# A gated linear attention's projections in tiles of 128 in place of 96, inside a fused transformer kernel on one Trainium2 core

## The reference

```python
q, k, v, g, lr, mq = split_cols(xn @ gla_w_in, (4*96, 4*96, 4*192, 4*192, 16, 256))
log_a = log_sigmoid(lr @ w_gate_up + b_gate) / 16            # a decay for each head, token and key feature
# 4 heads, 96 key features and 192 value features each
#   o_t = q_t * 96**-0.5 @ S_t,   S_t = exp(log_a_t) * S_(t-1) + k_t^T v_t
o = rmsnorm(o, out_norm) * silu(g)                           # the mean square is over a head's 192 values
mo = softmax(mq @ k_mem^T * 64**-0.5) @ v_mem                # 4 heads of 64 over 256 memory rows
h = h + concat(o, mo) @ w_out                                # (256, 768 + 256) @ (1024, 1024)
```

## Time and profile before

| | |
|---|---|
| time, median of 3 runs | 1646.41 us (1645.17 to 1646.71) |
| the profiled execution: its time | 1647.83 us |
| its span, first to last instruction | 1646.0 us |
| PE busy | 1518.2 us, 92% |
| DVE busy | 938.1 us, 57% |
| ACT busy | 414.1 us, 25% |
| GpSimd busy | 597.7 us, 36% |
| mean granted clock of TensorE | 0.989 |
| moved by DMA | 421.70 MB, mean 256 GB/s |

### The profile page before, as it was taken

One profiled execution on the slowest core, in us unless ns is written; L12 is line 12 of the kernel. 1 busy time (PEld: TensorE's weight loads), 2 busy tenths in 40 slices (PEclk: granted clock), 3 DMA queues, 4 the chain that ended last, 5 costly groups with the idle time before them and its releaser, 6 DMA issues. The chain is left out here.

```text
span 1646.0 us, 22237 instructions
## 1 busy us (share of the span) xinstructions
PE 1518.2 (92%) x7776; PEld 1138.2 (69%) x7778; DVE 938.1 (57%) x2383; ACT 414.1 (25%) x1007; POOL 597.7 (36%) x524
## 2 busy tenths in 40 slices
PE   7999989999999777778799999999999999999998
PEld 6998845554455323223357788999998878799997
DVE  5652576666766876766454732555553134555554
ACT  2120223213322222222124421111122145311112
POOL 4860233434333444434333103555521000455551
PEclk9999999999999999999999999999999999999999
DMA  8467699999999999999964135654424310555431
GB/s 326 162 224 158 244 428 387 427 426 427 427 420 426 423 427 427 427 426 397 426 282 153 52 128 219 213 169 162 153 106 133 121 52 1 205 169 168 162 127 38
DMA packets 64056, 421.70 MB, mean 256 GB/s; under 512 B 7456, under 2 KB 7904, under 8 KB 18432
## 3 DMA queue, kind: packets, MB, share of 16 engines
q0 software_dynamic: 38944, 277.19, 41.5%
q1 hardware_dynamic: 25024, 143.40, 24.3%
HBM read 416.12 MB, written 3.45 MB: 255 GB/s over the span
## 5 line engine op out<-in xcount | busy, mean ns | idle before, releaser
L2085 PE MATMUL wide<-arena 128*128 128x512 f32 x1024 | 475.4, 611 | 94.9 <-ACT arena L651 94.6
L2085 PEld LDWEIGHTS wide<-arena 128*128 128x128 f32 x1024 | 190.4, 193 | 357.4 <-issue 195.6
L1373 DVE CUSTOM_DVE_ANT_0 arena<-arena,wide 128x1024 f32<-128x1024 f32 x256 | 312.3, 1220 | 175.4 <-DMA arena<-uv_dram,arena 170.5
L494 POOL DMA_INDIRECT arena<-uv_dram,arena x256 | 260.0, 1016 | 406.1 <-PE wide L2085 288.4
L651 ACT ACTIVATE arena<-arena 128x2 f32<-128x2 f32 (+4 forms) x205 | 72.2, 354 | 507.1 <-DVE arena L1373 388.1
L2312 PE MATMUL wide<-arena,wring 128*128 128x256 f32 x704 | 158.6, 379 | 0.0
L1578 DVE SCALAR_TENSOR_TENSOR arena<-arena,prm 128x255 f32<-128x255 f32 (+1 forms) x152 | 126.0, 850 | 55.6 <-ACT arena L651 55.5
L2312 PEld LDWEIGHTS wide<-arena,wring 128*128 128x128 f32 x704 | 130.9, 190 | 16.2
L1612 DVE TENSOR_TENSOR arena<-bank,arena 128x128 f32<-128x128 f32 x266 | 73.9, 290 | 105.1 <-PE bank L2272 101.5
L651 ACT ACTIVATE arena<-bank 128x128 f32<-128x128 f32 (+7 forms) x102 | 41.7, 409 | 347.0 <-PE bank L2272 104.4
L505 POOL TENSOR_TENSOR arena<-arena 128x512 f32<-128x512 f32 x15 | 20.2, 1347 | 298.2 <-ACT arena L651 297.5
(11 more groups left out here) (275 smaller groups left out, 2126.4 us busy)
## 6 DMA issues: line engine op xcount, KB each, us to landing
wring<-ffn_dram SPq DMA_DIRECT2D x44, 1024.0 KB, 5.1
wring<-ffn_dram SPq DMA_DIRECT2D x44, 512.0 KB, 3.5
wring<-win_dram SPq DMA_DIRECT2D x15, 1024.0 KB, 5.4
wring<-wout_dram SPq DMA_DIRECT2D x8, 1024.0 KB, 9.3
wring<-wq_dram SPq DMA_DIRECT2D x5, 1024.0 KB, 7.5
wring<-wout_dram SPq DMA_DIRECT2D x4, 1280.0 KB, 5.5
wring<-mix_dram SPq DMA_DIRECT2D x4, 1024.0 KB, 5.3
arena<-uv_dram,arena POOLq DMA_INDIRECT x256, 11.8
```

Source lines behind the costliest of these rows:

```text
L494: pool.indirect_dma_start(out=G[:, n % NBUF, :], out_offset=None, in_=a["uv"], in_offset=bass.IndirectOffsetOnAxis(ap=idx[:, u, r:r + 1], ...
L1373: V.tensor_tensor_reduce(out=G[:, n % NBUF, 0:D], in0=G[:, n % NBUF, 0:D], in1=wide[:, 0:2, :].rearrange("p a b -> p (a b)"), scale=1.0, s ...
L2085: ins = MM(wide[:, 2 + h, :], diag[:, n % 4, e, :], G[:, r % NBUF, D + 512 * h:D + 512 * (h + 1)], start=r % (HEADS * TOPK) == 0, stop=r % ...
```

## The change

The four heads of 96 query features, and those of key features, are packed in three tiles of 128: heads 0, 1 and 2 take rows 0 to 95 of a tile each, and head 3 is cut into three parts of 32 that fill rows 96 to 127 of the three tiles. DVE moves head 3's parts to a tile of their own (partitions 96 to 127 to partitions 0, 32 and 64). The 768 gate values and values are reordered, the first 128 of each head, then the last 64 of heads 0 and 1 as one tile, and those of heads 2 and 3 as another: six tiles of 128 in place of eight of 96. The sums over the values give, for every head, one tile of 128 and one of which the half that belongs to the head (`lo`) is used. `w_out` has eight contraction tiles of 128 in place of ten.

So `glaqk` has 3 ring tiles of 1,024 KB in place of 4 of 768 KB, `glag` 3 of 1,024 in place of 4 of 768, and `wout0` 4 of 1,024 in place of 4 of 1,280. The order changes too: the first value projection comes ahead of the first pair product. `mean_squares` waits for both of ACT's squares, the roots go to SBUF (ACT frees the bank, no longer DVE), the reciprocal, products and gating of DVE go head by head, and the output projection takes contraction tiles 6, 7, 0 and 1 over all four output tiles first, and then tiles 2 to 5 for one output tile after the other.

```diff
-          ("memkv", 4, 2048), ("glalr", 1, 128), ("glaqk", 4, 1536), ("glamq", 1, 2048), ("glav", 2, 3072), ("glag", 4, 1536),
-          ("wout0", 4, 2560), ("ffn0", FT, 3072), ("kvc", 2, 2048), ("nsamq", 1, 2048), ("nsagl", 1, 288), ("nsaq", 3, 2048), ("kvs", 4, 2048),
+          ("memkv", 4, 2048), ("glalr", 1, 128), ("glaqk", 3, 2048), ("glamq", 1, 2048), ("glav", 2, 3072), ("glag", 3, 2048),
+          ("wout0", 4, 2048), ("ffn0", FT, 3072), ("kvc", 2, 2048), ("nsamq", 1, 2048), ("nsagl", 1, 288), ("nsaq", 3, 2048), ("kvs", 4, 2048),
...
-          ("gla_gate", 2, ACT_), ("mean_fin", 1, DVE_), ("gla_qk1", 3, ACT_), ("gla_p0", 2, DVE_), ("gla_v0", 1, ACT_), ("gla_mq", 1, ACT_), ("gla_p1", 2, DVE_),
+          ("gla_gate", 2, ACT_), ("mean_fin", 1, DVE_), ("gla_qk1", 2, DVE_), ("gla_v0", 1, ACT_), ("gla_p0", 2, DVE_), ("gla_mq", 1, ACT_), ("gla_p1", 2, DVE_),
...
-          ("gla_ms", 2, DVE_), ("gla_g2", 1, ACT_), ("gla_g3", 1, ACT_), ("wout0", 4, DVE_),
+          ("gla_ms", 2, ACT_), ("gla_g2", 1, ACT_), ("wout0", 4, DVE_),
...
-                copy(gg[:, 2 * i:2 * i + 2, :], halves(full(f"gla_g{i}"), DK), func=ACT.Silu).then_inc(freed[ACT_], 1)
+                copy(gg[:, 2 * i:2 * i + 2, :], halves(full(f"gla_g{i}")), func=ACT.Silu).then_inc(freed[ACT_], 1)
...
-            copy(gq[:, 2:4, :], halves(full("gla_qk1", 0), DK), scale=float(DK) ** -0.5).then_inc(freed[ACT_], 1)
-            copy(gk[:, 0:2, :], halves(full("gla_qk1", 1), DK)).then_inc(freed[ACT_], 1)
+            b = full("gla_qk1", 0)
+            copy(gq[:, 2, :], b[0:DK, 0:S], scale=float(DK) ** -0.5)
+            copy(gk[:, 0, :], b[0:DK, S:2 * S]).then_inc(qk_kept, 1)
+            copy(gk[:, 1:3, :], halves(full("gla_qk1", 1), DK)).then_inc(qk_kept, 1)
             decay(0)
+            keep_v(0)
             decay(1)
-            copy(gk[:, 2:4, :], halves(full("gla_qk1", 2), DK)).then_inc(freed[ACT_], 1)
             decay(2)
-            keep_v(0)
             copy(gmq, halves(full("gla_mq")), scale=0.125).then_inc(freed[ACT_], 1)
             decay(3)
...
-                copy(sqC[0:DK, 4 * n:4 * n + 4, :], wide[0:DK, 2 * n:2 * n + 2, :].rearrange("p a (b t) -> p (a b) t", b=2),
+                copy(sqC[:, 4 * n:4 * n + 4, :], wide[:, 2 * n:2 * n + 2, :].rearrange("p a (b t) -> p (a b) t", b=2),
                      func=ACT.Square).then_inc(g_sq, 1)
             keep_g(1)
             for i in range(2):
-                root("gla_ms", i, DK, 2 * S)
+                copy(rinv.rearrange("p (q i) t -> p i q t", i=2)[:, i], halves(full("gla_ms", i)), func=ACT.Sqrt, bias=eps[:]).then_inc(freed[ACT_], 1)
             keep_g(2)
-            keep_g(3)
...
             b = full("gla_qk0")
+            for m in range(2):
+                V.scalar_tensor_tensor(out=gq[32 * m:32 * m + 32, 3, :], in0=b[DK:128, m * S:(m + 1) * S], scalar=float(DK) ** -0.5,
+                                       in1=rstd[DK:128, :], op0=ALU.mult, op1=ALU.mult)
             V.tensor_tensor(halves(b, DK), halves(b, DK), rstd[0:DK, :].unsqueeze(1).broadcast_to([DK, 2, S]), ALU.mult).then_inc(scaled0, 1)
...
+            b = full("gla_qk1", 0)
+            dve.wait_ge(qk_kept, 1)
+            V.tensor_scalar(gq[64:DK, 3, :], b[DK:128, 0:S], float(DK) ** -0.5, None, ALU.mult)
+            V.tensor_copy(gk[0:32, 3, :], b[DK:128, S:2 * S]).then_inc(freed[DVE_], 1)
+            b = full("gla_qk1", 1)
+            dve.wait_ge(qk_kept, 2)
+            V.tensor_copy(gk[32:64, 3, :], b[DK:128, 0:S])
+            V.tensor_copy(gk[64:DK, 3, :], b[DK:128, S:2 * S]).then_inc(freed[DVE_], 1)
...
-                    dve.wait_ge(freed[ACT_], TAKEN[GROUP0["gla_qk1"] + 2])
+                    dve.wait_ge(freed[DVE_], TAKEN[GROUP0["gla_qk1"] + 1])
...
             for h in range(GH):
-                b = full("gla_ms", h // 2)
-                if h % 2 == 0:
-                    norm.n += 1
-                    dve.wait_ge(rooted, norm.n)
-                steps(V.reciprocal(rinv[:, h, :], b[0:DK, (h % 2) * S:(h % 2 + 1) * S]))
+                lo = 64 * (h % 2)
+                dve.wait_ge(freed[ACT_], TAKEN[GROUP0["gla_ms"] + h % 2])
+                steps(V.reciprocal(rinv[:, h, :], rinv[:, h, :]))
                 steps.join()
-                steps(V.tensor_tensor(gout[:, 2 * h:2 * h + 2, :], wide[0:DK, h, :].rearrange("p (b t) -> p b t", b=2),
-                                      rinv[:, h, :].unsqueeze(1).broadcast_to([DK, 2, S]), ALU.mult))
-                if h % 2:
-                    dve.drain().then_inc(freed[DVE_], 1)
-            steps.join()
-            for h in range(GH):
-                dve.wait_ge(freed[ACT_], TAKEN[GROUP0[f"gla_g{h}"]])
-                for v in range(2):
-                    j = 2 * h + v
-                    ins = V.scalar_tensor_tensor(out=gout[:, j, :], in0=gout[:, j, :], scalar=P("out_norm", v, rows=DK),
-                                                 in1=gg[:, j, :], op0=ALU.mult, op1=ALU.mult)
-                ins.then_inc(g_out, 1)
+                steps(V.tensor_tensor(gout[:, h, :], wide[:, h, 0:S], rinv[:, h, :], ALU.mult))
+                steps(V.tensor_tensor(gout[lo:lo + 64, 4 + h // 2, :], wide[lo:lo + 64, h, S:2 * S], rinv[lo:lo + 64, h, :], ALU.mult))
+                dve.wait_ge(freed[ACT_], TAKEN[GROUP0[f"gla_g{h // 2}"]])
+                steps.join()
+                V.scalar_tensor_tensor(out=gout[:, h, :], in0=gout[:, h, :], scalar=P("out_norm", 0), in1=gg[:, h, :],
+                                       op0=ALU.mult, op1=ALU.mult).then_inc(g_out, 1)
+            dve.wait_ge(freed[ACT_], TAKEN[GROUP0["gla_g2"]])
+            for j in range(4, 6):
+                V.scalar_tensor_tensor(out=gout[:, j, :], in0=gout[:, j, :], scalar=P("out_norm", 1), in1=gg[:, j, :],
+                                       op0=ALU.mult, op1=ALU.mult).then_inc(g_out, 1)
...
-                        cols = slice(h * DV + v * DK, h * DV + (v + 1) * DK)
+                        c0 = 128 * h if v == 0 else 512 + 128 * (h // 2)
+                        cols = slice(c0, c0 + 128)
                         o = v * S
-                        MM(wide[0:DK, h, o:o + 128], gv[:, 0, cols], pairs[:, 0, h, :], start=True, stop=True)
-                        MM(wide[0:DK, h, o + 128:o + 256], gv[:, 1, cols], pairs[:, 1, h, :], start=True, stop=False)
-                        ins = MM(wide[0:DK, h, o + 128:o + 256], gv[:, 0, cols], pairs[:, 2, h, :], start=False, stop=True)
+                        MM(wide[:, h, o:o + 128], gv[:, 0, cols], pairs[:, 0, h, :], start=True, stop=True)
+                        MM(wide[:, h, o + 128:o + 256], gv[:, 1, cols], pairs[:, 1, h, :], start=True, stop=False)
+                        ins = MM(wide[:, h, o + 128:o + 256], gv[:, 0, cols], pairs[:, 2, h, :], start=False, stop=True)
...
             def mean_squares():
-                for h in range(GH):
-                    pe.wait_ge(g_sq, h // 2 + 1)
-                    if h % 2 == 0:
-                        b = begin("gla_ms", h // 2)
-                    for v in range(2):
-                        ins = MM(b[0:DK, (h % 2) * S:(h % 2 + 1) * S], C("mean_dv", DK, rows=DK), sqC[0:DK, 2 * h + v, :],
-                                 start=v == 0, stop=v == 1)
-                    if h % 2:
-                        done(ins)
+                pe.wait_ge(g_sq, 2)
+                for i in range(2):
+                    b = begin("gla_ms", i)
+                    lo = 64 * i
+                    for q in range(2):
+                        h = 2 * q + i
+                        MM(b[:, q * S:(q + 1) * S], C("mean_dv", 128), sqC[:, 2 * h, :], start=True, stop=False)
+                        ins = MM(b[:, q * S:(q + 1) * S], cst[lo:lo + 64, CST["mean_dv"]:CST["mean_dv"] + 128],
+                                 sqC[lo:lo + 64, 2 * h + 1, :], start=False, stop=True)
+                    done(ins)
...
-            for i in range(3):
+            for i in range(2):
                 gla_qk("gla_qk1", i, i + 1)
-            pe.wait_ge(freed[ACT_], TAKEN[GROUP0["gla_qk1"] + 2])
+            gla_v(0)
+            pe.wait_ge(freed[DVE_], TAKEN[GROUP0["gla_qk1"] + 1])
             pair(0)
-            gla_v(0)
             done(project(slot("glamq", 0), hT, begin("gla_mq")))
...
-            gla_g(3)
+
+            def wout0(i, n):
+
+                k = (6, 7, 0, 1, 2, 3, 4, 5)[n]
+                if n == 0:
+                    begin("wout0", i)
+                    slot("wout0", i)
+                if k < 6:
+                    pe.wait_ge(g_out, k + 1)
+                b = bank[(GROUP0["wout0"] + i) % 4]
+                w = wring[:, (SLOT0["wout0"] + i) % RING, :]
+                src = gout[:, k, :] if k < 6 else moT[:, k - 6, :]
+                for m in range(2):
+                    o = (m * KT + k) * 128
+                    ins = MM(b[:, m * S:(m + 1) * S], w[:, o:o + 128], src, start=n == 0 and m == 0, stop=n == KT - 1 and m == 1)
+                if n == KT - 1:
```

(41 more changed lines are left out.)

12 lines of the change are left out of this document (3 added, 9 removed).

## The result

| | before | changed |
|---|---|---|
| median of 21 runs | 1653.81 us | 1640.11 us |
| ratio of the undisturbed executions, 95% interval | | 0.9922 (0.9903 to 0.9941) |
| executions of the lower group, median | 1646.19 us (9) | 1632.65 us (8) |
| executions of the upper group, median | 1655.36 us (11) | 1641.8 us (11) |

The change makes the kernel 0.8% faster, by 13.7 us between the medians, where 15.9 was forecast. The median of 1640.11 us lies outside the range of 1626 to 1635. Both kernels show two groups of times some 9 us apart; between the medians of the lower groups, and of the upper ones, the difference is 13.5 to 13.6 us. The lower group's median of 1632.65 us lies inside the range. The three runs shown ahead of the prediction (1645.17 to 1646.71) and their profiled execution (1647.83) were all of the lower group.

The account below looks back on a forecast made before the run. The prediction took TensorE's end-to-end matmuls to bound the GLA stage. Its terms, -21.4 + 0.6 + 0.8 + 0.15 + 2.3 + 1.7 = -15.9 us, took the median of 1646.41 to 1630.5 us, range 1626 to 1635.

Parts of the forecast that it names:

- 48 matmuls fewer: Key/query, gate and output projections: 16 matmuls fewer in each, at 0.432 us, 20.7 us removed.
- gap ahead of the first pair product: PE's 0.68 us wait for ACT's copy of the last keys goes, hidden under the first value projection: -0.7 us.
- larger first weight tile in the expert stage: Expert stage, DMA engines full: first weight tile grows from 768 to 1024 KB, +0.6 us (bounds 0 to 0.61).
- two DVE instructions ahead of the scaling: First queries: two 32x256 instructions out of PSUM delay DVE's scaling and everything behind, +0.8 us (bounds 0.7 to 0.9).
- sums over the values: 24 matmuls with 128-column weights, slightly dearer per record: +0.15 us; +1.75 if loads alone set the pace.
- mean squares: Still 8 matmuls, now waiting for both of ACT's squares, which finish under the gate projection: cost 0.
- wait for the fourth tile: Output projection: PE waits for wout0's fourth ring tile, requested only after the last gate projection: +2.3 us (2.2 to 2.7).
- low clock behind that wait: Output projection: one stretch at 1.2 GHz after PE's wait for the load, +1.7 us (0 to 3.4).
- low clock at the key projections, beside before's: Behind the gap near 865 us: before's 1.7 us loss counted as unchanged, range -1.7 to +1.7 us.
- The unit: One fp32 matmul with 256 moving columns takes 0.432 us, the same for 96 and 128 weight rows or columns.
- Rivals 3, 4 and 5: 3: decay chain sets level loop, 1637.4, 5%; 4: clock low through output projection, 1656.4, 2%; 5: no gain, 1646, 1%.
- rivals 1 and 2: 1: stall without low clock, 1628.8 or 1627.1 us, 17%; 2: second low-clock stretch or later landing, 1632.2 to 1634, 20%.

Follow-up runs that it names:

- tile by tile: Changed kernel with the output projection finishing one output tile after the other over all eight contraction tiles: 1632.31 us, ratio 0.9884.
- The whole-rows experiment: Changed kernel with the fourth output tile done whole last, plus the mean squares' second matmuls over all 128 rows against zero-padded constants: 1628.01 us, one execution.
- The execution on the other chip: Changed kernel, unaltered, profiled once more on another chip: 1639.21 us, span 1637.4.
- the two orders without the tile's wait: Changed kernel with the output projection finishing each output tile in turn (1632.31 us), or with only the fourth output tile done whole at the end (1632.83 us).

## Why the prediction was wrong

Its steps against the first profiled execution of the changed kernel:

| step | forecast | measured |
|---|---|---|
| 48 matmuls fewer | -20.7 | -20.74 |
| gap ahead of the first pair product | -0.7 | -0.68 |
| larger first weight tile in the expert stage | +0.6 | +0.60 |
| two DVE instructions ahead of the scaling | +0.8 | +0.92 |
| sums over the values | +0.15 | +0.13 |
| mean squares | 0 | +1.45 |
| wait for the fourth tile | +2.3 | +2.46 |
| low clock behind that wait | +1.7 | +1.74 |
| low clock at the key projections, beside before's | 0 | +1.05 |
| sum | -15.9 | -13.1 |

The -20.74 are 48 x 0.432; two groups of 32 records at 6.91 us and the projection's 27.79 in place of 34.72 (tile by tile, without the wait) give -20.75. The rows in the stage add up to -13.7, and the stage got 13.58 us shorter; the other 0.1 is in the first queries, whose 32 records take 3.74 us with 128 weight columns and took 3.66 with 96. The 0.6 us lie ahead of the stage. There the step from the experts' dot product at 781.71 us to the next at 786.63 is 4.92 us, 4.33 before; it is 4.91 to 4.93 in seven of the eight executions with the larger tile (4.64 in the eighth, whose next step is 0.3 longer), and 4.32 and 4.12 in the two others with the smaller one.

**The step that failed is the last**, the base to which the sum was added: "It ran 1.4 us above the median of the runs, which goes to 1646.41 - 15.9". It took three runs for the level of the kernel. All three were of the lower group, and about half of all executions of before lie some 9 us higher. The profiled ones of these have the long low stretch of the second layer, at a place that the change doesn't touch. That all three fell in the lower group was bad luck; that the range left the other group out was the fault. With the working as it stood, the median of before of the result, 1653.81, would have given 1637.9; the lower group's 1646.19 gives 1630.3, where the changed kernel's lower group has 1632.65. So 7.4 of the 9.6 us of the miss are this base, and 2.2 the sum, which gave -15.9 where the groups moved by 13.5 to 13.6.

**Mean squares were mis-sized**: "Mean squares keep 8 matmuls" is right, but not their price. The unit was read from neighbours with equal rows. The change makes a 128-row and a 64-row matmul alternate, and seven steps of 0.627 less 0.432 are 1.37, the first 0.09. The whole-rows experiment takes it away. The forecast put this term at 0 and gave it no upper bound, though its trace held no such alternation to read a price from.

**The clock in front** was counted as unchanged, with a range of -1.7 to +1.7. The execution on the other chip has no low clock there at all; the term varies by chance between executions, and +1.05 is what this one drew.

**What was right.** The unit of 0.432 us holds for 128 rows and 128 weight columns throughout, as it did for 96. The Trainium skill (TensorE: Matmul & The Clock Gate, LDWEIGHTS) lets a load cost by its columns; if loads had set the pace, the sums over values would have taken 7.0 us; they take 5.37 (942.98 to 948.34), so the loads lie under the matmuls. The keys, decay, subtraction and gating are all hidden: the level loop from the memory queries to the gate projection takes 47.01 us, 46.99 before. The wait at the fourth tile, its releaser and its length came as worked out, and removing it returned it (4.1 us with the low stretch). That a low stretch follows it is right for one execution and not for the other. Rivals 3, 4 and 5 did not occur; rivals 1 and 2 are two outcomes of the same chance, and both occurred: a second stretch in one execution, none in the other.

**What stays open.** Why the second layer's stretch comes in one execution and not in the next, and whether the changed kernel is drawn to it more often (19 of 28 against 31 of 62). In four of the seven profiled executions that have the change and the old order here, PE stands 0.45 to 0.99 us ahead of the 68 columns, in neither of before; three of these four have no long stretch. Open is also why the six runs each of the two orders without the tile's wait reach only 1634.61 and 1637.14, so that their gain over the changed kernel beside them (9.8 and 9.3 us between medians) is larger than the 4.1 us seen in the stage. Seven of that kernel's eight runs there were of the upper group, which may be part of it; the runs here do not say more.

## What to carry to other kernels

Before a forecast is turned into a time, look at how the executions of the kernel scatter: three runs that agree within 0.1% can all be of one group, and a range has to hold the other. When a matmul's shape changes, look at its neighbours as well: a constant padded with zeros, so that all eight matmuls of a group have 128 rows, was 1.45 us cheaper than having every second one with 64. When an order of use over ring slots is changed, work out for each tile the time from its request to its first use; finishing three tiles before touching the fourth costs nothing and removed a wait of 2.3 to 2.5 us.

## What the runs showed of the hardware

- The granted clock fell to 1.2 GHz in or after TensorE's gaps of 0.9 to 2.5 us in some executions and not in others, on the same gap of the same kernel (1.83 us: 16.70 or 14.05 us for the 64 records behind it).
- A low clock lasted 17 to 20 us in four executions, in three of them without any gap of TensorE: it stayed at 1.2 GHz through 64 records of 68 columns, and 7.8 to 9.8 us were lost. In the profiled execution with 32 records of 256 columns in their place it was back within these.
- Fp32 matmuls of 256 columns with 128 and 64 rows in turn step by 0.627 us, those with 128 rows alone by 0.432; with 64 rows alone, eight records take 1.07 us.
- A copy or scaling of 32 rows and 256 columns out of PSUM to other partitions takes VectorE 0.42 to 0.43 us, about as much as the 0.44 of a scaling of 128 rows and 254 columns: here fewer rows were no cheaper.
